# When x's second token half is loaded and normalised, and how the first modulation section becomes columns

## The reference

```
mod = silu(c) @ w_ada + b_ada          # nine sections of 1024: sh1, sc1, gt1, sh2, ...
h = rmsnorm(x) * g_ffn1 * (1 + sc1) + sh1
x = x + 0.5 * gt1 * ((silu(h @ w1) * (h @ w3)) @ w2)
x = x + gt2 * mixer(modulated rmsnorm of x)        # attention heads and short convolution
x = x + 0.5 * gt3 * (second SwiGLU of the modulated rmsnorm)
out = modulated rmsnorm(x)                          # with w_ada_final
```

## Time and profile before

| | |
|---|---|
| Time, median of 3 runs | 1903.11 us (1902.67 to 1903.18) |
| The profiled execution | 1910.78 us, span in the profile 1909.0 us |
| PE busy | 1839.2 us, 96% of the span |
| DVE / ACT / POOL busy | 66% / 41% / 14% |
| Matmuls of the plain group start | 44.58 us after the span's start |
| TensorE's granted clock, mean | 0.986 |

### The profile page before, as it was taken

How to read it: one execution, slowest core, us unless ns; L and a number is a source line. 1 busy time by engine, 2 the same in 40 slices (tenths; PEclk the granted TensorE clock), 3 DMA queues, 4 the chain that set the end, 5 groups by cost and what they waited for, 6 DMA issues and landing times.

```text
span 1909.0 us, 22939 instructions
## 1 busy us (share of the span) xinstructions
PE 1839.2 (96%) x8248; PEld 1469.2 (77%) x8248; DVE 1263.6 (66%) x1955; ACT 777.4 (41%) x1395; POOL 270.4 (14%) x411
## 2 busy tenths in 40 slices
PE   5999999999999999999999999899999999999997
PEld 2878888888888877888876666787888888878885
DVE  5887777777576776434236667687667766567767
ACT  4643333333344564111125555564333333344445
POOL 2011211211220000000303330101111211112000
PEclk9999999999999999999999899999999999999998
DMA  8165565654864321111201110325454544476432
GB/s 315 68 232 191 203 220 184 234 202 166 272 214 150 98 79 64 35 51 38 78 28 39 45 34 1 133 84 203 155 193 166 200 159 166 159 262 217 128 99 88
DMA packets 100528, 269.76 MB, mean 141 GB/s; under 512 B 13120, under 2 KB 13504, under 8 KB 100288
## 3 DMA queue, kind: packets, MB, share of 16 engines
q1 hardware_dynamic: 62608, 146.30, 22.2%
q0 software_dynamic: 34304, 117.46, 18.0%
q10 hardware_dynamic: 3504, 4.53, 1.0%
HBM read 209.53 MB, written 54.53 MB: 138 GB/s over the span
## 4 chain that ended last, share of the span: by engine, by line
PE 84%; DVE 8%; ACT 4%; issue 2%; DMA 1%; ACTq 1%; POOL 1%; DVEq 0%; POOLq 0%
PE PS L1538 59%; PE PS L1534 24%; DMA AdaFirst<-ada 1%; PE PS L1953 1%; ACTq L871 1%; DVE X L1105 1%; DVE NMax L1445 1%; DVE Ml L1244 1%; ACT X L670 0%; DVE SqSum L1310 0%; DVE TmpA L1328 0%; DVE Wl L1004 0%; DVE Wl L1039 0%; ACT PR L893 0%; DVE Wl L1036 0%
## 5 line engine op out<-in xcount | busy, mean ns | idle before, releaser
L1538 PE MATMUL PS<-Bh,Wh 128*128 128x512 f32 x1120 | 441.5, 394 | 3.7 <-ACT T L653 3.7
L1538 PE MATMUL PS<-Bl,Wh 128*128 128x512 f32 x1120 | 440.6, 393 | 0.0
L1538 PE MATMUL PS<-Bh,Wl 128*128 128x512 f32 x1120 | 440.0, 393 | 0.0
L1538 PEld LDWEIGHTS PS<-Bh,Wh 128*128 128x128 f32 x1120 | 209.8, 187 | 55.9 <-issue 3.9
L1538 PEld LDWEIGHTS PS<-Bh,Wl 128*128 128x128 f32 x1120 | 209.8, 187 | 50.1
L1538 PEld LDWEIGHTS PS<-Bl,Wh 128*128 128x128 f32 x1120 | 209.8, 187 | 48.9
L1538 PE MATMUL PS<-Wh 128*128 128x512 f32 x616 | 240.3, 390 | 3.4 <-DVE Wl L1039 1.7
L1538 PE MATMUL PS<-Wh,Wl 128*128 128x512 f32 x616 | 239.7, 389 | 0.0
L1538 PE MATMUL PS<-Wl,Wh 128*128 128x512 f32 x616 | 239.7, 389 | 0.0
L1036 DVE TENSOR_TENSOR Wl<-RawB,Wh 128x512 fp32r<-128x512 f32 x154 | 106.6, 692 | 136.4 <-ACT Wh L628 135.2
L628 ACT ACTIVATE Wh<-RawB 128x512 fp32r<-128x512 f32 x154 | 97.3, 632 | 230.0 <-PE PS L1538 230.0
(11 more groups left out here) (188 smaller groups left out, 2883.0 us busy)
## 6 DMA issues: line engine op xcount, KB each, us to landing
Raw<-up_w SPq DMA_DIRECT2D x86, 512.0 KB, 5.3
Ada<-ada POOLq DMA_DIRECT2D x72, 512.0 KB, 4.3
g_dram<-T SPq DMA_DIRECT2D x88, 256.0 KB, 2.1
W2s<-down_w POOLq DMA_DIRECT2D x88, 256.0 KB, 4.5
s_dram<-W2s POOLq DMA_DIRECT2D x88, 256.0 KB, 2.5
GQ<-g_dram POOLq DMA_DIRECT2D x88, 256.0 KB, 3.3
RawB<-s_dram SPq DMA_DIRECT2D x88, 256.0 KB, 2.8
RawB<-down_w SPq DMA_DIRECT2D x66, 256.0 KB, 2.8
```

Source lines behind the costliest of these rows:

```text
L1538: return nc.tensor.matmul(out, lhs, rhs, start=first, stop=last, skip_group_check=True)
```

## The change

- x's second token half is no longer loaded first. SP loads it in four pieces once piece 3 of AdaFirst has landed; POOL loads nothing of it. SP starts the first up weights already when piece 1 of AdaFirst has landed.
- The norm of the second half moves into the plain group. ACT squares tiles 0 and 1 behind chunk 1, tiles 2 and 3 behind chunk 2, tiles 4 to 7 behind chunk 3 (and behind the preparation of weight slots 4 and 5), and takes the root behind chunk 5. POOL adds the squares (`late_sums(1)`). PE makes `mean(1)` ahead of chunk 5 and `bcast(1)` ahead of chunk 6. DVE spreads at chunk 5 and normalises tiles 8 and 9 at chunk 6, 10 to 12 at chunk 7, 13 to 15 at chunk 8.
- `second_cols(1)` moves from ahead of chunk 3 to ahead of chunk 4; the tiles of DVE's second column half are spread 3, 3, 2 over chunks 1 to 3 instead of 4, 2, 2.
- Section sh1 is made as columns: each 128 by 128 block of AdaFirst is the weight, and silu(c) the one moving column: 8 products for each of 8 tiles, straight into bank 4. The row, its copy on ACT and the turning products are gone, and with them the waits on `row_done`.

```
         def sums_of(q, d):
-            if q == 5:
-                return late_sum, d
-            return ssum, (KT - 1) * (q - (q > 5)) + d
+            if q in (1, 5):
+                return late_sum, (KT - 1) * (q // 5) + d
+            return ssum, (KT - 1) * (q - (q > 1) - (q > 5)) + d
...
-            for h in range(NH):
-                for c in (0, 2):
-                    load_x_first(sp, h, c)
-
-            sp.wait_ge(first_loaded[2], 16)
+            for c in (0, 2):
+                load_x_first(sp, 0, c)
+            sp.wait_ge(first_loaded[1], 16)
             for u in range(2):
                 for f in range(GF):
                     sp.dma_start(Raw[:, 2 * u + f, 0, :], ...)
+            sp.wait_ge(first_loaded[3], 16)
+            for c in range(KT // 2):
+                load_x_first(sp, 1, c)
...
+            def late_sums(q):
+                for d in range(1, KT):
+                    pool.wait_ge(sq_done, q * KT + d + 1)
+                    if d >= 2:
+                        pool.wait_ge(*sums_of(q, d - 1))
+                    nc.gpsimd.tensor_tensor(SqSum[:, 1, :], SqSum[:, 1, :], Sq[:, d % 2, :], ALU.add).then_inc(late_sum, 1)
...
+            late_sums(1)
             block_of(0)
...
                     b_chunk(ph, c)
+                    for k in {1: (0, 1), 2: (2, 3)}.get(c, ()) if ph == 0 else ():
+                        square_first(1, k)
                     if ph == 0 and c in (KH - 1, KH):
                         for o in ((4, 5), (6, 7))[c - KH + 1]:
                             prep_hi(0, o)
+                    if ph == 0 and c == KH - 1:
+                        for k in range(4, KT):
+                            square_first(1, k)
+                    if ph == 0 and c == KH + 1:
+                        root(1)
...
-            root(1)
-            act.wait_ge(row_used, KT)
-            nc.scalar.activation(AdaRow[0:1, :], flat(PS[0:1, 0:2, :]), ACT.Copy).then_inc(row_done, 1)
...
-                        for k in {1: (0, 1, 2, 3), 2: (4, 5), 3: (6, 7)}.get(c, ()):
+                        for k in {1: (0, 1, 2), 2: (3, 4, 5), 3: (6, 7)}.get(c, ()):
                             second_tile(k, 1)
+                        if c == 3:
+                            nm(0, KH)
+                            second_scale(1)
...
+                        if 3 <= c < 6:
+                            nm(0, c + 2)
+                        if c == 5:
+                            spread(1)
+                        for k in {6: (8, 9), 7: (10, 11, 12), 8: (13, 14, 15)}.get(c, ()):
+                            nm(0, k)
...
-                        if ph == 0 and h == 0 and k == KH - 1:
+                        if ph == 0 and h == 0 and k == KH:
                             second_cols(1)
+                        elif ph == 0 and h == 0 and k == KH + 1:
+                            mean(1)
+                        elif ph == 0 and h == 0 and k == KH + 2:
+                            bcast(1)
...
             for k in range(KT):
                 pe.wait_ge(first_loaded[k // 2], 16)
-                for c in range(D // HALF):
-                    made = mm(PS[0:1, c, :], CAct[:, k:k + 1], AdaFirst[:, k, half(c)], k == 0, k == KT - 1)
-                made.then_inc(row_used, 1)
-                if k == 1:
+                for c in range(KT):
+                    made = mm_open(PS[:, 4, c:c + 1], AdaFirst[:, k, blk(c)], CAct[:, k:k + 1], k == 0 and c == 0, k == KT - 1)
+                if k == 3:
                     pe.wait_ge(square_loaded, 16)
                     bcast(0)
-                elif k == 3:
-                    pe.wait_ge(root_done, 1)
-                    mean(1)
-                elif k == 5:
-                    bcast(1)
+            made.then_inc(cols_done, 1)
             second_cols(0)
-            pe.wait_ge(row_done, 1)
-            for c in range(KT):
-                made = mm(PS[:, 4, c:c + 1], AdaRow[0:1, blk(c)], Ones[0:1, :], True, True)
-            made.then_inc(cols_done, 1)
```

More of the change, by code:

```diff
@@ L199, in program @@
         AdaSum0, _ = place("AdaSum0", [P, D], like=t_at)
-        AdaRow, _ = place("AdaRow", [P, D], like=t_at + 4 * K)
         Lam4, _ = place("Lam4", [P, 4, DH], like=t_at + 8 * K)
@@ L353, in program @@
         mset, consts, c_act = sem("mset"), sem("consts"), sem("c_act")
-        ada_used, row_used, row_done = sem("ada_used"), sem("row_used"), sem("row_done")
+        ada_used = sem("ada_used")
         cols_done, mod_done, scales = sem("cols_done"), sem("mod_done"), sem("scales")
@@ L498, in _ @@
         def _(pool):
-            for h in range(NH):
-                for c in (1, 3):
-                    load_x_first(pool, h, c)
+            for c in (1, 3):
+                load_x_first(pool, 0, c)
             def load_second(c, n):
@@ L583, in _ @@
                 body(hh, True)
[L585 to L589, removed]
+            late_sums(5)
             block_of(1)
@@ L804, in square_first @@
                 if k >= 3:
-                    act.wait_ge(ssum, (KT - 1) * h + k - 2)
+                    act.wait_ge(*sums_of(h, k - 2))
                 elif k and h:
-                    act.wait_ge(ssum, KT - 1)
+                    act.wait_ge(*sums_of(0, KT - 1))
                 out = Sq[:, k % 2, :] if k else SqSum[:, h, :]
@@ L812, in _ @@
                 square_first(0, k)
-            for k in range(KT):
-                square_first(1, k)
-                if k == 1:
-                    root(0)
-            root(1)
-            act.wait_ge(row_used, KT)
-            nc.scalar.activation(AdaRow[0:1, :], flat(PS[0:1, 0:2, :]), ACT.Copy).then_inc(row_done, 1)
+            root(0)
             for o in range(4):
@@ L1125, in up @@
                     if ph == 0:
-                        for k in {1: (0, 1, 2, 3), 2: (4, 5), 3: (6, 7)}.get(c, ()):
+                        for k in {1: (0, 1, 2), 2: (3, 4, 5), 3: (6, 7)}.get(c, ()):
                             second_tile(k, 1)
+                        if c == 3:
+                            nm(0, KH)
+                            second_scale(1)
                         for o in {3: (4, 5), 4: (6, 7)}.get(c, ()):
[L1130 to L1136, removed]
+                            prep_lo(0, o)
+                        if 3 <= c < 6:
[4 more added lines that the diff above has]
+                            nm(0, k)
                 plain_mul(ph, 0)
@@ L1274, in second_bias @@
             def second_bias(n):
-                dve.wait_ge(cols_done, 2 * n + 1)
+                dve.wait_ge(cols_done, n + 2)
                 a = SC1 * KT + KH * n
@@ L1283, in second_scale @@
                     second_bias(n)
-                dve.wait_ge(mod_done, 2 * n + 1)
+                dve.wait_ge(mod_done, n + 2)
                 a = SC1 * KT + KH * n
@@ L1289, in ada_bias @@
             def ada_bias(s, bank=7):
-                dve.wait_ge(cols_done, s + 2 if s else 2)
+                dve.wait_ge(cols_done, s + 2 if s else 1)
                 nc.vector.tensor_tensor(Mod[:, bass.ts(s, KT)], PS[:, bank, 0:KT], Cols[:, bass.ts(s, KT)], ALU.add)\
@@ L1355, in _ @@
             nc.vector.tensor_reduce(LamS[:, 0:2], LamP[:], AX.X, ALU.add).then_inc(lam_done, 1)
[L1356 to L1369, removed]
+            for k in range(1, KT):
+                add_squares(0, k)
+            dve.wait_ge(lam_exp, 1)
+            nc.vector.tensor_tensor(LamS[:, 4:5], LamS[:, 3:4], LamS[:, 2:3], ALU.subtract).then_inc(lam_done, 1)
+            dve.wait_ge(lam_done, 3)
+            nc.vector.tensor_scalar(LamS[:, 5:6], LamS[:, 4:5], -LAMBDA_INIT, None, ALU.add).then_inc(lam_done, 1)
+            nc.vector.tensor_scalar(SubG[:], col("subln"), 1.0 - LAMBDA_INIT, None, ALU.mult).then_inc(lam_done, 1)
+            spread(0)
             for k in range(KT):
@@ L1375, in _ @@
                     nm(0, 1)
-                    spread(1)
                 elif k == 5:
@@ L1379, in _ @@
                     nm(0, 3)
+            ada_bias(SH1, 4)
             second_bias(0)
-            ada_bias(SH1, 4)
             second_scale(0)
@@ L1580, in plain_free @@
                         pe.wait_ge(evac, EVAC["end"])
-                    elif ph == 0 and j == 0:
-                        pe.wait_ge(row_done, 1)
                 elif j == 0:
```

## The result

The first comparison gave 1925.16 us (median of 4, 1919.32 to 1927.81) against 1903.14 before (median of 4): ratio 1.01, 95% interval 1.008 to 1.0119. A second one gave 1923.81 (median of 6) against 1905.6 (median of 23): ratio 1.0096, interval 1.0077 to 1.0115. The forecast was 1917.7, the range 1905 to 1921: the sign was right, the loss was forecast too small (14.6 us against 22.0 and 18.2), and both times lie outside the range.

A forecast was written before the change was run, and what follows sets the result against it. Two things set the time: when the last columns are made and when ACT ends chunk 15. 7.2 (front) + 6.7 (plain group) + 0.7 (clock) = 14.6 us on 1903.1 gave 1917.7, range 1905 to 1921.

The forecast's parts named there:

- The front: Start up to the last columns: 128 one-column instructions at 1.2 GHz, 28.5 us, end at 48.5 instead of 41.24, +7.2 us.
- The plain group: Chunks 0 to 15, from the group's first matmul: ACT ends chunk 15 at 36.1 instead of 29.35, +6.7 us.
- second_cols(1): Behind chunk 3's 12 matmuls: ACT's chunk 4 begins 2.85 us later, PE waits 2.7 us bare ahead of chunk 4.
- The norm inside: In the plain group: ACT's root waits 2.5 us for PE's mean(1), chunk 8 waits 1.5 us for bcast(1) and DVE.
- Hidden: ... POOL's seven additions.: In the plain group: additions at 1.27 to 1.55 us end 7 us ahead of mean(1), so they cost nothing.
- rival 3: POOL's additions beside DVE take twice as long, mean(1) slips 3 us: +17.6, 1920.7 us; chance 0.05.
- The clock: Around chunk 4: 3.6 us without 512-column work may lower PE's clock; ends 0 and 1.5 (a second spell: 3), taken +0.7 us.
- Passing on: Behind the plain group: ACT's chunk delay goes through in full; a delay of PE's alone would first fill 3.3 us of waiting.
- rival 2: ACT and DVE have slack behind the plain group, only PE's delay less 3.3 us counts: +8.8, 1911.9 us; chance 0.08.
- rival 1: The column stream gets the full clock, 0.1225 us an instruction: middle +1, 1904 us; chance 0.16.
- rival 4: Small instructions overlap better in the long stream, 0.18 instead of 0.2225 us: +9.2, 1912.3 us; chance 0.05.
- The sum's footing: The base time: 1903.1 us, the median of the runs, to which the sum of 14.6 us was added.

The follow-up runs named there:

- e1: The changed kernel with section sh1 made as a row again (32 instructions of 512 columns, copy, turning): 1913.52 us, 1.0041 of the kernel before.
- e2: The kernel before with section sh1 made as columns and nothing else: 1915.47 us, 1.0059 of the kernel before.
- e5: The changed kernel with four thrown-away 512-column float32 products behind each tile of the column stream: 1942.68 us, 1.0194 of the kernel before.
- e4: The changed kernel with POOL's seven additions cut to 8 columns and second_cols(1) back ahead of chunk 3: 1914.10 us, 1.0046 of the kernel before.
- e3: The changed kernel with POOL's seven additions of norm 1 over 8 columns instead of 512: 1919.19 us, 1.0076 of the kernel before.
- e11: The kernel before with ten unused 128x512 additions on POOL beside the first four chunks: 1911.78 us, 1.0046 of the kernel before.

## Why the forecast came out too small

**Where the miss lies.** Forecast 14.6, measured 22.0 at the medians of the first comparison. Up to M it is 18.0: the front 1.7 less than forecast, the plain group 5.1 more (3.4 more by the second profile, where M is 16.1 later). The other 4.0 lie behind M, where the mean granted clock is what differs.

**The front: mechanism right, size near.** Forecast +7.2, measured +5.5. The stream did run at 1.2 GHz from end to end (e1, e2 and e5 show it from three sides). It took 27.2 us (13.65 and 13.51) and not 28.5, 1.3 less: I had divided the 1.78 us of mean(0)'s loads by eight, but the next instruction starts 1.70 us behind mean(0)'s first (14.04 to 15.74), 0.2125 each. A start at 15.74 and not 16.1, and a bcast(0) of 1.85 and not 2.1, make up the rest. The Trainium skill's sentences ("TensorE: Matmul & The Clock Gate", "Why this matters for your kernels") that continuous work brings the full clock would have given the stream the full clock; this case's trace disagrees: PE and PEld were busy without a gap for 30 us, and every instruction took the low clock's time. Beyond that no run here shows what sets the level.

**The plain group: 12.5 behind S, forecast 6.7 + 0.7.** The experiments take it apart: 5.3 for having the norm inside (e4 against before, 11.0 - 5.7), 2.7 for second_cols(1) behind chunk 3 (e3 against e4), 4.4 for POOL's additions (changed against e3), or 2.7 by the second profile of the changed kernel, in which the group lost 10.8.
- second_cols(1): forecast 2.85, measured 2.7; PE's bare wait 2.7, measured 2.86. Right.
- The norm inside: forecast 2.5 + 1.5 for ACT's two waits. In e4 they are 2.34 and 1.43. The term came out at 5.3; 1.0 to 1.2 us of it are the longer spell at 1.2 GHz at the start of the group (chunk 0 took 5.3 us in e4, 4.3 before), and e2 has the same 1.2 with the norm ahead of the group. So the waits themselves were forecast right.
- **The step that failed: "Hidden: ... POOL's seven additions."** I asked whether POOL would be late and whether DVE would slow POOL, and priced that as rival 3. POOL was not late; it slowed DVE. DVE's second tiles were not ready by S + 8.5 but by S + 14.75, PE waited 1.82 us ahead of chunk 3, and second_cols(1) stood at S + 15.2 and not S + 12.7. By e3 this cost 2.7 to 4.4 us where the sum had nothing: 1.4 by DVE itself, the rest by the clock in chunk 4 and behind the group. The trace of before showed it: I read POOL's durations in the only stretch with such additions and not DVE's beside them. There the low part of a weight slot, 0.68 us otherwise, takes 1.12 beside one of POOL's additions (and 1.19 beside another, at 1235.51):

```profile
1227.36 0.68 DVE L1004 TENSOR_TENSOR Wl<-Raw,Wh 128x512 fp32r<-128x512 f32 x1
1227.64 1.55 POOL L589 TENSOR_TENSOR SqSum<-SqSum,Sq 128x512 f32<-128x512 f32 x1 [0.64 <-ACT Sq L769]
...
1228.62 1.12 DVE L1004 TENSOR_TENSOR Wl<-Raw,Wh 128x512 fp32r<-128x512 f32 x1
```

The Trainium skill states this contention: "SBUF — State Buffer", section "SBUF: two separate sides", has DVE instructions with two SBUF inputs and GpSimd's exclude each other from a shared port for a whole instruction, and "GPSIMD Engine Reference", section "Specifications", names the contention. e3 and e11 agree (0.75 against up to 1.8 us; the form that reads PSUM untouched). This rule spoke against the change and I did not weigh it.
- The clock, the second term that was too small: forecast 0.7, bounds 0 to 3. Chunk 4 took 5.3 instead of 2.8 us, 2.5 more (1.5 more in the second profile), and the work behind 116.49 was slow once more. I had taken half a fall of 1.5 us. The one long wait that I had priced, 2.86 us ahead of chunk 4, brought no fall in chunk 4 in e3; with the unforecast 1.82 us ahead of chunk 3 as well there was one. This is no further loss: the experiments count it with POOL's additions.

**Passing on.** That ACT's delay goes through in full and PE's 3.3 us of waiting do not absorb it (against rival 2) held: ACT ended chunk 15 17.4 us later (91.32) and M came 18.0 later. PE's wait behind the group grew to 4.04 us. In the changed kernel ACT's root waited 4.80 us for PE and not 2.5, since mean(1) stood behind the slow chunk 4; chunk 8 waited 1.43, as forecast. Rivals 1, 2, 3 and 4 did not come true. Rival 3 named +17.6, near the 18.0 at M, but by luck: it made POOL late for mean(1), and POOL was 11 us early.

**The sum's footing.** 1903.11 stood on three runs; the same kernel gave medians of 1901.0 to 1906.0 later, following the clock in its attention part. The 18.0 and 16.1 at M against 22.0 and 18.2 at the medians are of that size. Why the changed kernel's runs had rather low mean clocks (0.986 to 0.990) is open; part of it is the falls within its own first 125 us.

No kernel tried was shown to beat the one before.

## What to carry to other kernels

Look at what a rearranged product does to the weight loads and at the clock it will run at: here turning 16 wide products into 64 one-column ones saved a copy and a transposition, but each instruction cost its weight load, the stream ran at 1.2 GHz from end to end, and 11 us were lost on the same DMA loads. Before giving an idle POOL an elementwise job, look at what DVE does in the same microseconds; if it reads two operands from SBUF there, the job may be paid on DVE's list, as it was here, so search the trace for both engines' durations side by side. Work ahead of a pipelined stretch can be free where the same work inside it is not: once the norm had moved among the chunks, each hand-over between PE, ACT and DVE in it showed as a wait (2.34 and 1.43 us in e4).

## What was not expected of the hardware

- DVE's TENSOR_SCALAR with a single SBUF operand was slowed too, 1.50 instead of 0.48 us beside POOL's additions (e11).
- POOL's own additions grew as well: up to 1.84 us in the changed kernel, 1.65 on average in e11 (16.46 / 10), where 1.27 is the least seen.
- The kernel before moves by 12 us from run to run (1900.5 to 1912.8 us) with the mean granted clock (0.993 to 0.985); three runs within 0.5 us of one another did not show it.
